# Gate rows of both gated layers: six ones-by-diagonal products and their copies replaced by rows kept in a DRAM scratch and read back repeated on all partitions

## The reference

```
for layer in (0, 1):
    mod_l = silu(c) @ w_ada[layer] + b_ada[layer]          # 6 * 1024 values
    mod_c = silu(c_ctx) @ w_ada[layer] + b_ada[layer]
    sh1, sc1, g1, sh2, sc2, g2 = split(mod, 6)              # for each stream
    y_l, y_c = even_mixer(...) or odd_mixer(...)            # of modulate(x, sh1, sc1)
    x_l = x_l + g1_l * y_l
    x_l = x_l + g2_l * conv_ffn(modulate(x_l, sh2_l, sc2_l), ...)
    if layer == 0:
        x_c = x_c + g1_c * y_c
        x_c = x_c + g2_c * conv_ffn(modulate(x_c, sh2_c, sc2_c), ...)
```

## Time and profile before

| | |
|---|---|
| time, median of 3 runs | 2065.58 us (2064.91 to 2069.85) |
| span of the profiled execution, which is its own time | 2060.8 us |
| TensorE: matmul, weight load | 98%, 70% of the span |
| VectorE, ScalarE, GpSimd | 57%, 20%, 1% |
| granted TensorE clock | above 0.9 in each of 40 slices |
| moved by DMA | 292.68 MB, mean 142 GB/s |

### The profile page before, as it was taken

The page is one execution under the profiler, slowest core; times in us unless marked ns, Lnnn a source line. Parts: engine busy times, 40 slices in busy tenths (PEclk is TensorE's granted clock), DMA queues, the critical chain, the costliest instruction groups (busy, mean ns, idle before and its releaser), DMA issues.

```text
span 2060.8 us, 25000 instructions
## 1 busy us (share of the span) xinstructions
PE 2020.9 (98%) x10844; PEld 1436.7 (70%) x10844; DVE 1172.6 (57%) x1651; ACT 403.6 (20%) x831; POOL 10.7 (1%) x22
## 2 busy tenths in 40 slices
PE   8999999999999999999999999999999999999998
PEld 7787766984486599446864557988884466559973
DVE  4664785654464475544435854455555674637776
ACT  3313111000222301113112642111110112321110
POOL 0000000000000000000000000000000000000000
PEclk9999999999999999999999999999999999999999
DMA  5635694454353244443232002122223443123442
GB/s 205 245 124 189 273 374 193 169 187 195 122 205 133 93 182 176 169 150 121 82 122 82 1 0 83 71 93 86 102 99 148 190 178 143 41 81 143 176 153 103
DMA packets 22909, 292.68 MB, mean 142 GB/s; under 512 B 2784, under 2 KB 3040, under 8 KB 5008
## 3 DMA queue, kind: packets, MB, share of 16 engines
q1 hardware_dynamic: 21024, 280.67, 36.0%
q0 software_dynamic: 1776, 10.43, 1.4%
HBM read 290.03 MB, written 1.05 MB: 141 GB/s over the span
## 4 chain that ended last, share of the span: by engine, by line
PE 90%; DVE 6%; DMA 2%; ACT 1%; issue 0%; SPq 0%; DVEq 0%; ACTq 0%
PE bank L325 88%; DMA ring<-in_W 2%; DVE small L857 1%; PE bank L688 1%; DVE arena L878 1%; PE bank L781 0%; DVE arena L699 0%; DVE arena L642 0%; DVE arena L852 0%; ACT arena L815 0%; DVE arena L871 0%; DVE arena L598 0%; DVE arena L2654 0%; DVE HT L2526 0%; ACT arena L697 0%
## 5 line engine op out<-in xcount | busy, mean ns | idle before, releaser
L325 PE MATMUL bank<-arena 128*128 128x128 f32 (+10 forms) x3840 | 668.9, 348 | 7.0 <-DVE arena L1658 1.4
L325 PEld LDWEIGHTS bank<-arena 128*128 128x128 f32 (+4 forms) x3840 | 469.2, 183 | 189.1 <-issue 148.6
L325 PE MATMUL bank<-HT,ring 128*128 128x128 f32 (+1 forms) x2448 | 407.9, 325 | 5.5 <-DMA ring<-in_W 3.1
L325 PEld LDWEIGHTS bank<-HT,ring 128*128 128x128 f32 x2448 | 363.4, 192 | 45.7 <-issue 8.9
L325 PE MATMUL bank<-ring,arena 128*128 128x512 f32 (+1 forms) x674 | 295.5, 593 | 0.6 <-ACT arena L697 0.6
L325 PEld LDWEIGHTS bank<-ring,arena 128*128 128x128 f32 (+1 forms) x674 | 127.2, 190 | 155.8 <-issue 155.1
L325 PE MATMUL bank<-ring,HT 128*128 128x512 f32 (+2 forms) x512 | 193.9, 536 | 1.0 <-ACT HT L2022 0.8
L325 PE MATMUL bank<-arena,ring 128*128 128x128 f32 (+4 forms) x1158 | 187.3, 323 | 0.1
L325 PEld LDWEIGHTS bank<-arena,ring 128*128 128x128 f32 (+3 forms) x1158 | 165.6, 190 | 15.1 <-issue 2.2
L325 PEld LDWEIGHTS bank<-ring,HT 128*128 128x128 f32 x512 | 90.5, 194 | 98.3 <-issue 95.2
L697 ACT ACTIVATE arena<-bank 128x512 f32<-128x512 f32 (+2 forms) x126 | 68.9, 575 | 439.4 <-PE bank L325 436.0
(11 more groups left out here) (307 smaller groups left out, 1554.8 us busy)
## 6 DMA issues: line engine op xcount, KB each, us to landing
ring<-in_W SPq DMA_DIRECT2D x125, 2048.0 KB, 7.8
ring<-in_W SPq DMA_DIRECT2D x6, 1536.0 KB, 8.8
ring<-in_W SPq DMA_DIRECT2D x4, 1024.0 KB, 9.1
arena<-in_rel POOLq DMA_DIRECT2D x1, 2048.0 KB, 11.1
arena<-in_rpb POOLq DMA_DIRECT2D x1, 2048.0 KB, 9.6
arena<-in_dft POOLq DMA_DIRECT2D x2, 640.0 KB, 6.5
X<-in_x SPq DMA_DIRECT2D x2, 512.0 KB, 6.0
X<-in_ctx POOLq DMA_DIRECT2D x1, 1024.0 KB, 5.0
```

Of the source, the lines that this page charges most:

```text
L325: return nc.tensor.matmul(out_, lhsT, rhs, start=start, stop=stop, skip_group_check=True)
```

## The change

All gates are turned at once. In the first mixer's output projection, between tile 0 and tile 1 of the second half, TensorE makes two products, one for each layer: the 64 columns of `MOD` that hold the gates (32 groups, of which 16 are gates, times two streams) as the stationary side, the identity as the moving one. The result is 64 rows of 128 values for each layer, in one bank. ScalarE copies it to `ADR` at the end of `act_eout`. Four DMAs of the POOL queue, issued when that stage is done and ahead of the ple0 loads, write the gate rows of both layers to a DRAM scratch `gate_rows` of 32 KB in pieces of 512 bytes. Two more POOL DMAs read it back repeated on all 128 partitions: `gates(0, 2)`, four rows, 2 MB at the destination, behind the bias table of the even mixer and a product mark in its first weight block; `gates(1, 1)`, two rows, 1 MB, as the last one behind the tables of the odd mixer. VectorE waits for these ahead of the residual sums of `wout` and `oout`, where it waited for ScalarE's copies. The diagonals, the six pairs of ones-products and the twelve copies are gone. `GT_` and all that reads it stay.

```diff
+        gate_rows = nc.dram_tensor("gate_rows", (2, 2, 2, KT, P), F32, kind="Internal").ap()
...
-        def pe_gate(i, s, j):
-            pe.wait_ge(vector_done, at(f"diag{i}.{s}.{j}"))
-            for h in range(2):
-                ps = open_bank(f"gate{i}.{s}.{j}.{h}")
-                mm(ps[:, :], K("ones"), DG[:, 4 * h:4 * h + 4, :], True, True).then_inc(tensor_done, pe.one())
-                pe.mark(f"gate{i}.{s}.{j}.{h}")
-
-        def act_gate(i, s, j):
-            for h in range(2):
-                copy_out(act, f"gate{i}.{s}.{j}.{h}", GT_[:, s, j, h * 512:(h + 1) * 512])
-            act.mark(f"gate out{i}.{s}.{j}")
-
-        def dve_gate(i, s, j, before=None):
-
-            m = (2, 5)[j]
-            if before:
-                dve.wait_ge(tensor_done, at(f"gate{before}.1"))
-            tt(DG, rows(K("ident"), 8), bc(MOD[:, i, 8 * m:8 * m + 8, s], [P, 8, P]), ALU.mult).then_inc(vector_done, dve.one())
-            dve.wait_ge(vector_done, dve.n)
-            dve.mark(f"diag{i}.{s}.{j}")
+        GROW = [[ADR[48 * j:48 * j + 16, i * P:(i + 1) * P] for j in range(2)] for i in range(2)]
+
+        def pe_gate_rows():
+            pe.wait_ge(vector_done, at("mod1 ready"))
+            ps = open_bank("gate rows")
+            for i in range(2):
+                cols = MOD[:, i, 16:48, :].rearrange("p m s -> p (m s)")
+                last = mm(ps[0:64, i * P:(i + 1) * P], cols, K("ident"), True, True)
+            last.then_inc(tensor_done, pe.one())
+            pe.mark("gate rows")
+
+        def act_gate_rows():
+            ps = full(act, "gate rows")
+            activation(ADR[0:64, 0:2 * P], ps[0:64, 0:2 * P], ACT.Copy).then_inc(scalar_done, act.one())
+            act.mark("read gate rows", "gate rows out")
...
                 pe.mark(f"vn.{t}")
                 if t == 0:
-                    pe_gate(0, 0, 0)
                     spread("qd")
                     spread("kd")
-            pe_gate(0, 0, 1)
             rotate("qd", QD5)
...
             rotate("kd", KD5)
-            pe_gate(0, 1, 0)
...
                 if t == 1:
-                    pe_gate(0, 1, 1)
                     spread("qn")
                     spread("kn")
...
             pe_feature_block("hin2", "hu", m0=8, after={0: lambda: next_layer(1), 1: lambda: next_layer(2)})
-            pe_gate(1, 0, 0)
...
                 pe_rotate("g7", [QK7[:, j, :] for j in range(5)])
-                pe_gate(1, 0, 1)
...
-            dve.wait_ge(scalar_done, at("gate out0.1.1"))
+            dve.wait_ge(loaded["gates"], at("gates 0"))
             for t in range(4):
                 dve_add("wout", 0, [t], gate_row(0))
...
             dve_pairs("gqa", gqa_steps, PB7, between={1: lambda: long(0), 2: lambda: long(1)})
-            dve.wait_ge(scalar_done, at("gate out1.0.1"))
+            dve.wait_ge(loaded["gates"], at("gates 1"))
...
+            def gates(i, n):
+                load("gates", GT_[:, 0:n].rearrange("p s j d -> p (s j d)"), gate_rows[i, 0:n].rearrange("s j k c -> (s j k c)").unsqueeze(0).broadcast_to([P, n * 2 * D]))
+                group["gates"].mark(f"gates {i}")
+
             for i in range(2):
                 after("eout" if i == 0 else "attn")
+                if i == 0:
+                    for n in range(2):
+                        for j in range(2):
+                            load("rows", gate_rows[n, :, j].rearrange("s k c -> k s c"), GROW[n][j])
+                    group["rows"].mark("rows kept")
...
             group["bias"].mark("bm loaded")
+            e.wait_ge(tensor_done, at("win 1 p1.4"))
+            e.wait_ge(loaded["rows"], at("rows kept"))
+            gates(0, 2)
             after("ffn0")
...
             group["odd"].mark("rope7 in", "hyena in")
+            gates(1, 1)
```

More of the change, by code:

```diff
@@ L175, in row_plan @@
     return out, at
-LOADS = ("x0", "x1", "ident", "colp", "const", "start", "mix_rows", "ctx", "ple0", "rel", "ple1", "even", "bias", "odd")
+LOADS = ("x0", "x1", "ident", "colp", "const", "start", "mix_rows", "ctx", "ple0", "rel", "ple1", "even", "bias", "odd", "rows", "gates")
 CPLAN, NCOL = column_plan()
@@ L1070, in dve_mod @@
             dve.wait_ge(vector_done, dve.n)
+            dve.mark(f"mod{i} ready")
         def pe_lora_up():
@@ L2023, in act_eout @@
                     act.mark("read " + n)
+            act_gate_rows()
         def dve_eout():
@@ L2051, in pe_eout @@
                             pe.mark(f"eout{o}.{t}")
+                    if h == 1 and t == 0:
+                        pe_gate_rows()
         def mlp_places():
@@ L2743, in build @@
         JK5 = BM.rearrange("p a b c -> p (a b c)")[:, 2 * D:4 * D].rearrange("p (a b) -> p a b", a=2)
-        DG = arena[:, AR - 1024:AR].rearrange("p (a b) -> p a b", a=8)
         YD = BM.rearrange("p a b c -> p (a b c)")[:, 0:2048].rearrange("p (t c) -> p t c", t=4)
@@ L2929, in act_even @@
             copy_out(act, "vn.0", VN[:, 0, :])
-            act_gate(0, 0, 0)
             act.wait_ge(vector_done, at("win 1 joined1"))
@@ L2935, in act_even @@
                     squares(*(("qn", QN), ("kn", KN))[t - 1])
-            act_gate(0, 0, 1)
             act_norm_root("qn5", INVE["qn"])
@@ L2942, in act_even @@
             act.mark("read lam", "lam exp")
-            act_gate(0, 1, 0)
             for t in range(4):
                 copy_out(act, f"vd.{t}", VD5[:, t, :])
-                if t == 1:
-                    act_gate(0, 1, 1)
             act.wait_ge(scalar_done, act.n)
@@ L3006, in dve_even @@
             dve.wait_ge(vector_done, dve.n)
-            dve_gate(0, 0, 0)
             normed("qd", QD5, "da_q")
             normed("kd", KD5, "da_k")
-            dve_gate(0, 0, 1, "0.0.0")
             dve.wait_ge(loaded["even"], at("rope in"))
             dve_rotate("qd", QD5[:, :, 0:SEQ], 4, RC, ROT5)
-            dve_gate(0, 1, 0, "0.0.1")
             dve.wait_ge(vector_done, dve.n)
@@ L3017, in dve_even @@
             dve_norm_inverse("kn5", INVE["kn"])
-            dve_gate(0, 1, 1, "0.1.0")
             normed("qn", QN, "na_q")
@@ L3226, in act_odd @@
             sine(2)
-            act_gate(1, 0, 0)
             for j in range(2):
@@ L3242, in act_odd @@
             hu_out(0)
-            act_gate(1, 0, 1)
             hu_out(1)
@@ L3258, in dve_odd @@
                 dve_unit("mod o", t, four(XN7[:, t % 2, :]))
-            dve_gate(1, 0, 0)
             tmp = junk512[0:64, 0:SEQ]
@@ L3305, in dve_odd @@
             dve.mark("z fm")
-            dve_gate(1, 0, 1, "1.0.0")
             dve.wait_ge(loaded["odd"], at("hyena in"))
```

## The result

The changed kernel takes 2054.99 us (median of 4 runs, 2054.09 to 2055.83); the kernel before, in the same comparison, 2066.04 us (4 runs, 2064.91 to 2069.85). The ratio is 0.9949, with a 95% interval of 0.9936 to 0.9963, so 0.5% faster: the medians lie 11.05 us apart, the interval is 7.6 to 13.2 us. Forecast were 2056.4 us and a range of 2053.5 to 2060.5. A second comparison, on 7 runs against 12, gave 2057.47 against 2065.07, ratio 0.996 (0.9945 to 0.9975). The gain is real and lies between 5 and 13 us; the traces say more exactly where it is.

A forecast was written before the change was run, and what follows sets the result against it. TensorE was taken as the bound (busy 2020.9 of 2060.8 us, 90% of the chain). Savings of 10.45 us less losses of 1.3 gave a gain of 9.2: span 2051.6, median 2056.4, range 2053.5 to 2060.5 us.

The forecast's parts named there:

- All four gates as forecast: Even mixer: removing the gate products saves 1.8, 1.7, 2.0 and 1.8 us, 7.3 us in all.
- the third: Even mixer, gate behind the rotation of kd: 2.0 us saved, 1.7 of products and a wait of 0.3.
- the wait of 0.3: Behind the rotation of kd, TensorE's wait for VectorE's diagonal, 0.3 us, was to go with the gate.
- The rival that the spreads give it back: Even mixer: two spreads wait longer for ScalarE's tile copy, both 1.8 us savings vanish; gain 5.6, 2060.0 us; chance 0.07.
- the 0.51 us ahead of the second spread: Even mixer, behind vn.0: the second norm spread, at 1062.15, was said to have waited for ScalarE's copy of the gate.
- the wait for hu.1 moved to the second score pair: Odd mixer, second gate: the second score pair, no longer the convolution, waits for VectorE's read of hu.1; 0.85 us saved.
- +0.8 in the band: Band attention: the first score pair reopens v1.0's bank and waits for ScalarE's copy; 0.8 us lost.
- -0.6 at oout: First half of the odd output projection: it gets a bank free earlier, so its 0.56 us wait goes; 0.6 us saved.
- The additions: Gate-row products in the first output projection cost 0.5 us; ScalarE's copy, row DMAs and both broadcasts cost nothing.
- 1119: Even mixer: the heads begin at 1119 us, VectorE needs the first broadcast behind them; landing forecast by 1094 at the latest.
- The rivals in which it holds up the tables: First filter product waits for tables delayed by the second broadcast: 3.3 us, 2059.7 (chance 0.11), or 20.5 us, 2076.9 (0.04).
- the 4.8 us between span and median: Whole kernel: the median of the runs stays 4.8 us above the profiled execution's span, carried along as a constant.

The follow-up runs named there:

- The version with hu.1 apart: The changed kernel with hu.1, the last tile ahead of the odd heads' attention, in bank 5 instead of 3, the counter still moving on; 2059.43 us.
- the version with the shift alone: The kernel before with only the bank counter moved on by one in the first mixer's output projection, no product added; 2061.40 us.
- the version with the counter kept: The changed kernel with the gate rows' bank opened by number, so the bank counter does not move there; 2056.07 us.

## Why the prediction was right

**The price of a product.** TensorE's instruction at 0.429 us was right, so 1.72 us for a gate row: the steps read at five of the six gates are 1.7 us each, or 1.7 and a wait. At the 131 ns of the Trainium skill's page "TensorE: Matmul & The Clock Gate", section "Back-to-back issue gap", a gate row would, by an estimate, have been worth 0.5 us, and none was. Shown.

**The even mixer.** All four gates as forecast within 0.1 us except the third, 2.3 in place of 2.0. I had taken the wait of 0.3 for the diagonal and four instructions; the products behind the rotation now also start before it is drained, which I had not counted. The rival that the spreads give it back is refuted: the spread behind vn.0 shows its old gaps. One of these the prediction had read wrongly: the 0.51 us ahead of the second spread it put down to ScalarE's copy of the gate, and they stand there without a gate too.

**The odd mixer.** The mechanism was right, the wait for hu.1 moved to the second score pair; it saved 0.65 in place of 0.85 because the pair takes 1.06 us up to the convolution and not 0.86. The version with hu.1 apart shows that the bank alone holds back the rest.

**The banks.** +0.8 in the band and -0.6 at oout were right, and the version with the shift alone shows both without the change. What the forecast did not see is that the shift alone would also have freed the convolution: 1.6 us in the odd mixer need no gate row at all. The changed kernel has only the 0.6 of them, since there hu.1 comes to lie in a bank that the second pair reopens.

**The additions.** The gate rows cost 0.65 us of TensorE, not 0.5. That ScalarE's copy costs nothing was right at its place and wrong by 0.28 us some 240 us later. The first broadcast landed 15.0 us after its issue, well ahead of 1119, and the second in 9.2 behind the tables. The rivals in which it holds up the tables need it in front of them; there they are real, at 2.9 us of idle time and 3.1 more by the clock. (1024 KB at 306 GB/s are 3.4 us, not the 3.3 of the prediction; nothing hangs on it.)

**Span and median.** The sum by place, 8.8 read against 9.2 forecast, is right; that the 4.8 us between span and median would stay is wrong, as told above. That the median forecast came within 1.4 us is in part luck, since two errors offset each other: 3 us too many for what lies around the span, and a fall of the clock, 1.5 us, that I had not foreseen in the span. The distance of the medians, 11.05 us in one comparison and 7.6 in the other, carries such falls too, and is no finer test of the 9.2.

## What to carry over

Where a counter hands out buffers, taking out or adding one call is a second change: list which tile now lies in which bank and who reopens it, because a shift by one was worth +0.8, -1.0 and -0.6 us here, and putting one tile aside gave 2.1 us more. A broadcast that has time belongs behind the transfers that something waits for, never in front of them. And when the differences are below 0.5%, compare traces place by place: one run at half clock for 14 us hid a gain of 2 us that the trace showed at once.

## What was unexpected of the hardware

The falls of the clock to 1.2 GHz told of so far came behind idle times of TensorE of 0.85 to 3.30 us, and cost from about two thirds of the idle time to about twice as much: 1.5 us behind 2.33, 3.1 us behind 3.30, 6.4 us behind 3.11. Behind the shortest, in the second trace of the kernel before, sixteen products took 3.55 us that had taken 1.96:

```profile
304.78 3.55 PE L325 MATMUL bank<-arena 128*64 128x128 f32 x16 [0.85 <-DVE arena L1658]
```

These falls are not repeated from run to run (the same gap of 2.05 us was followed by 2.0 us and by 3.35 us for the same sixteen products). The times of the kernel before go with the mean granted clock: 2061.3 to 2064.0 us in the later runs at 0.996, 2069.0 to 2070.3 at 0.992 and 0.993; that such falls make this scatter is likely, but only profiled executions show where the clock fell.

An idle time is neither enough nor needed. A gap of 3.01 us near 212, in the version with the counter kept, and one of 1.2 us near 1200, in all 13 traces, were followed by no fall. And in all 13 traces the clock falls near 162 us, for 6.8 us in twelve of them and for 3.4 in one, with no idle time of TensorE in the 10 us ahead. There it makes products of 2 and of 8 columns. Timeline of the kernel before, and its busy time up to the fall and in it:

```profile
158.72 1.84 PE L325 MATMUL bank<-KC,arena 128*128 128x2 f32 x16
160.42 4.94 PE L325 MATMUL bank<-ring,HT 128*128 128x8 f32 x32
```

```profile
158.00:162.60 4.60, 4.60 (x41) 4.50 (x39) 2.61 (x6) 2.30 (x4) 0.00 (x0) 1.00 0.57 178
162.67:169.50 6.83, 6.83 (x34) 6.83 (x34) 1.18 (x2) 4.04 (x5) 0.00 (x0) 0.50 0.91 338
```

One more instruction on ScalarE, 0.38 us long, made a copy 240 us later start 0.28 us later in each of the nine traces that had it; why is open.
